# Modulation rows of PE copied by ACT and added in the column sums, loads in three parts, first column block formed by DVE and rounded from there

## What is computed

```python
c_act = jax.nn.silu(c)
mod = (c_act @ w_ada + b_ada)[:, None, :]
shift, scale, gate = jnp.split(mod, 3, axis=-1)
u = layer_norm(x) * (1 + scale) + shift
proj = u @ w_in + b_in
...
```

## Time and profile before

| what | us |
|---|---|
| median of 3 runs | 2171.29 |
| lowest and highest run | 2171.26, 2171.71 |
| the profiled execution | 2171.44 |
| its span, first to last instruction | 2169.3 |
| PE busy in the span | 2144.8 (99%) |
| PE weight loads busy | 1769.2 |
| DVE busy | 1270.0 |
| ACT busy | 784.7 |

### The profile page before, as it was taken

The page is one execution under the profiler, slowest core; times in us unless marked ns, Lnnn a source line. Parts: engine busy times, 40 slices in busy tenths (PEclk is TensorE's granted clock), DMA queues, the critical chain, the costliest instruction groups (busy, mean ns, idle before and its releaser), DMA issues.

```text
span 2169.3 us, 24997 instructions
## 1 busy us (share of the span) xinstructions
PE 2144.8 (99%) x10371; PEld 1769.2 (82%) x10371; DVE 1270.0 (59%) x1668; ACT 784.7 (36%) x1043; POOL 27.7 (1%) x41
## 2 busy tenths in 40 slices
PE   7999999999999999999999999999999999999998
PEld 4888888888888887888888888888788888888887
DVE  6899897944665848434665554234843466555423
ACT  3323232223343354344353333135534334333312
POOL 1000000000000100000000000000000000000000
PEclk9999999999999999999999999999999999999999
DMA  9432232232232222322223232222232222323322
GB/s 312 148 117 83 97 102 83 97 116 97 97 102 97 97 78 78 130 65 92 84 81 114 80 113 100 88 76 90 78 124 71 86 90 78 111 84 109 104 89 78
DMA packets 181364, 217.86 MB, mean 100 GB/s; under 512 B 3836, under 2 KB 152964, under 8 KB 180996
## 3 DMA queue, kind: packets, MB, share of 16 engines
q1 hardware_dynamic: 178000, 209.47, 29.2%
q10 hardware_dynamic: 2804, 4.65, 0.6%
q0 software_dynamic: 448, 2.15, 0.3%
HBM read 212.06 MB, written 4.19 MB: 100 GB/s over the span
## 4 chain that ended last, share of the span: by engine, by line
PE 96%; DVE 2%; DMA 1%; ACT 1%; issue 0%; POOL 0%; SPq 0%; POOLq 0%; ACTq 0%; DVEq 0%
PE psum L1790 30%; PE psum L1792 30%; PE psum L1791 30%; PE psum L2191 1%; DMA ada<-in_w_ada 1%; PE psum L2223 1%; PE psum L2203 1%; DVE whl L516 1%; PE psum L2157 1%; PE psum L2144 0%; PE psum L2176 0%; PE psum L1814 0%; POOL stat L677 0%; DVE hT L1474 0%; PE psum L2161 0%
## 5 line engine op out<-in xcount | busy, mean ns | idle before, releaser
L1790 PE MATMUL psum<-hT,whl 128*128 128x512 f32 (+1 forms) x2064 | 789.2, 382 | 3.3 <-DVE hT L1178 1.7
L1792 PE MATMUL psum<-hT,whl 128*128 128x512 f32 (+1 forms) x2064 | 783.2, 379 | 0.0
L1791 PE MATMUL psum<-hT,whl 128*128 128x512 f32 (+1 forms) x2064 | 783.0, 379 | 0.0
L516 DVE TENSOR_TENSOR whl<-raw,whl 128x1024 fp32r<-128x1024 f32 x361 | 438.2, 1216 | 430.8 <-ACT whl L509 430.6
L509 ACT ACTIVATE whl<-raw 128x1024 fp32r<-128x1024 f32 x362 | 377.7, 1047 | 425.1 <-PE psum L1792 385.6
L1790 PEld LDWEIGHTS psum<-hT,whl 128*128 128x128 f32 x2064 | 388.2, 188 | 84.6 <-issue 7.1
L1792 PEld LDWEIGHTS psum<-hT,whl 128*128 128x128 f32 x2064 | 388.3, 188 | 73.8
L1791 PEld LDWEIGHTS psum<-hT,whl 128*128 128x128 f32 x2064 | 388.4, 188 | 71.7 <-issue 0.2
L1790 PE MATMUL psum<-whl,ff 128*128 128x512 f32 x352 | 137.1, 389 | 0.0
L1792 PE MATMUL psum<-whl,ff 128*128 128x512 f32 x352 | 136.9, 389 | 0.0
L1791 PE MATMUL psum<-whl,ff 128*128 128x512 f32 x352 | 136.9, 389 | 0.0
(11 more groups left out here) (320 smaller groups left out, 2159.5 us busy)
## 6 DMA issues: line engine op xcount, KB each, us to landing
raw<-in_w_in SPq DMA_DIRECT2D x88, 1024.0 KB, 5.1
raw<-in_w_up SPq DMA_DIRECT2D x44, 1024.0 KB, 5.1
raw<-in_w_down SPq DMA_DIRECT2D x20, 1024.0 KB, 5.0
ada<-in_w_ada SPq DMA_DIRECT2D x12, 1024.0 KB, 10.9
raw<-in_w_branch SPq DMA_DIRECT2D x12, 1024.0 KB, 4.9
raw<-in_w_out SPq DMA_DIRECT2D x12, 1024.0 KB, 5.0
x<-in_x SPq DMA_DIRECT2D x4, 512.0 KB, 6.2
v_by_token<-vnat ACTq DMA_DIRECT2D x4, 512.0 KB, 3.0
```

The lines of the kernel that those rows point to most:

```text
L516: nc.vector.tensor_tensor(whl_view(w, 1), raw_view(w), whl_view(w, 0).bitcast(F), ALU.subtract).then_inc(w_lo, 1)
L1790: M(out_, stat_hi, mov_hi, start=start, stop=False, **kw)
L1791: M(out_, stat_hi, mov_lo, start=False, stop=False, **kw)
L1792: return M(out_, stat_lo, mov_hi, start=False, stop=stop, **kw)
```

## The change

Four things change together.

1. PE's row no longer goes into `adsum`. ACT copies it from PSUM into `table[0:1, i % 2, :]` (`row_copy`), and `ada_columns` adds it there: after each matmul of 128 rows a second one follows on the same PSUM column, whose weights are 128 columns of that single row and whose moving operand is one number. DVE's addition (L1153) goes. All four rows now use the same PSUM partition, so `ada_product(i)` waits until the row before has been copied.
2. PE's share of row groups by block goes from 3, 5, 3, 3 to 4, 4, 2, 3 in the order 0, 2, 1, 3.
3. Each block comes in three loads, `k` 0 to 3, 4 and 5, 6 and 7, each with its own semaphore, and DVE waits for them one by one.
4. For column block 0 DVE forms the full value first (`u_whole`, semaphore `first_u`), ACT rounds it from `utmp` to the high part, and DVE subtracts. ACT does its part of block 1 after that.

```diff
-    PE_ROWS = {0: 3, 2: 5, 1: 3, 3: 3}
+    PE_ROWS = {0: 4, 2: 4, 1: 2, 3: 3}
...
-                for q in (2 * b, 2 * b + 1):
-                    k0, n0 = q % 2 * 4, b * SEQ
-                    sp.dma_start(ada[:, q, :].rearrange("p (k n) -> p k n", k=4), wa[:, k0:k0 + 4, n0:n0 + SEQ]).then_inc(s_ada[q], 16)
+                both = ada[:, 2 * b:2 * b + 2, :].rearrange("p q (k n) -> p (q k) n", k=4)
+                for i, (k0, k1) in enumerate(((0, 4), (4, 6), (6, 8))):
+                    sp.dma_start(both[:, k0:k1, :], wa[:, k0:k1, b * SEQ:(b + 1) * SEQ]).then_inc(s_ada[b][i], 16)
...
+            def row_copy(i):
+
+                act.wait_ge(arow_ps, i + 1)
+                A(table[0:1, i % 2, :], bank(7)[0:1, :], ACT.Copy).then_inc(s_arow, 1)
...
+                if ct == 0:
+                    act.wait_ge(s_u0, 1)
+                    A(hT[:, 0, 0, :], utmp[:, 0, :], ACT.Copy).then_inc(h_hi, 1)
+                    return
...
-                weighted(part, lambda k: ada_rows(b, k), range(PE_ROWS[b], KT)).then_inc(s_part, 1)
-                dve.wait_ge(s_part, i + 1)
-                dve.wait_ge(arow_ps, i + 1)
-                own = part[32 * b:32 * b + 1, :]
-                V.tensor_tensor(own, own, bank(7)[32 * b:32 * b + 1, :], ALU.add).then_inc(s_adsum, 1)
+                for k in range(PE_ROWS[b], KT):
+                    if k == PE_ROWS[b] and k < 4:
+                        dve.wait_ge(s_ada[b][0], 16)
+                    if k in (4, 6):
+                        dve.wait_ge(s_ada[b][k // 2 - 1], 16)
...
+                ins.then_inc(s_adsum, 1)
...
+                if i:
+                    pe.wait_ge(s_arow, i)
...
                 pe.wait_ge(s_adsum, i + 1)
+                pe.wait_ge(s_arow, i + 1)
                 for m in range(4):
-                    ins = M(bank(6)[:, 4 * b + m:4 * b + m + 1], adsum[:, 2 * b + m // 2, m % 2 * P:(m % 2 + 1) * P], negones[:, 0:1],
-                            start=True, stop=True)
+                    o_ = bank(6)[:, 4 * b + m:4 * b + m + 1]
+                    M(o_, adsum[:, 2 * b + m // 2, m % 2 * P:(m % 2 + 1) * P], negones[:, 0:1], start=True, stop=False)
+                    ins = M(o_, table[0:1, i % 2, m * P:(m + 1) * P], negones[0:1, 0:1], start=False, stop=True)
```

More of the change, by code:

```diff
@@ L387, in build @@
         s_vec, s_vec2, s_cst, s_cst2, s_adag, s_bcast = (sem(n) for n in ("vec_in", "vec2_in", "cst_in", "cst2_in", "adag_in", "bcast_in"))
-        s_ada = [sem(f"ada_in{q}") for q in range(8)]
+        s_ada = [[sem(f"ada_in{b}_{i}") for i in range(3)] for b in range(TB)]
         s_c, s_cT, u_act = sem("c_in"), sem("c_transposed"), sem("u_by_act")
-        arow_ps, s_part, s_nmr, s_xc = sem("ada_row_psum"), sem("ada_part"), sem("neg_mean_rstd"), sem("x_columns")
+        arow_ps, s_arow, s_u0, s_nmr, s_xc = sem("ada_row_psum"), sem("ada_row_copied"), sem("first_u"), sem("neg_mean_rstd"), sem("x_columns")
         s_vT, s_vcol, s_mod, s_modc, s_gp, s_gate = (sem(n) for n in ("vecT", "vcol_ready", "mod_psum", "modc_ready", "gate_psum", "gate_ready"))
@@ L705, in _ @@
                 A(xn1[:, tb, :], x[:, tb, :], ACT.Identity, bias=nmr[:, tb:tb + 1], scale=rstd[:, tb:tb + 1]).then_inc(s_xn, 1)
+            def row_copy(i):
+                act.wait_ge(arow_ps, i + 1)
+                A(table[0:1, i % 2, :], bank(7)[0:1, :], ACT.Copy).then_inc(s_arow, 1)
+            row_copy(0)
             act.wait_ge(s_vT, 6)
@@ L711, in _ @@
             A(halfb[:, 96:128], vcol[:, VOFF["b_gate"]:VOFF["b_gate"] + 32], ACT.Copy, scale=0.5).then_inc(s_ini, 1)
+            row_copy(1)
             split_hi(0)
             def columns_hi(ct):
+                if ct == 0:
+                    act.wait_ge(s_u0, 1)
+                    A(hT[:, 0, 0, :], utmp[:, 0, :], ACT.Copy).then_inc(h_hi, 1)
+                    return
                 act.wait_ge(s_xc, ct + 1)
@@ L728, in _ @@
             columns_hi(3)
-            for w in range(2, 6):
-                split_hi(w)
+            split_hi(2)
+            split_hi(3)
+            row_copy(2)
+            split_hi(4)
+            split_hi(5)
+            row_copy(3)
             act.wait_ge(s_modc, 2)
@@ L1144, in ada_sum @@
                 b = MOD_ORDER[i]
-                if PE_ROWS[b] < 4:
-                    dve.wait_ge(s_ada[2 * b], 16)
-                dve.wait_ge(s_ada[2 * b + 1], 16)
                 part = adsum[:, 2 * b:2 * b + 2, :].rearrange("p a b -> p (a b)")
-                weighted(part, lambda k: ada_rows(b, k), range(PE_ROWS[b], KT)).then_inc(s_part, 1)
-                dve.wait_ge(s_part, i + 1)
-                dve.wait_ge(arow_ps, i + 1)
-                own = part[32 * b:32 * b + 1, :]
-                V.tensor_tensor(own, own, bank(7)[32 * b:32 * b + 1, :], ALU.add).then_inc(s_adsum, 1)
+                for k in range(PE_ROWS[b], KT):
[3 more added lines that the diff above has]
+                        dve.wait_ge(s_ada[b][k // 2 - 1], 16)
+                    if k == PE_ROWS[b]:
+                        ins = V.tensor_scalar(part, ada_rows(b, k), cact[:, k:k + 1], None, ALU.mult)
+                    else:
+                        ins = V.scalar_tensor_tensor(part, ada_rows(b, k), cact[:, k:k + 1], part, ALU.mult, ALU.add)
+                    if k < KT - 1:
+                        link(ins)
+                ins.then_inc(s_adsum, 1)
             def modulation(h):
@@ L1166, in u_whole @@
                 dve.wait_ge(s_xc, ct + 1)
-                if ct >= 2:
-                    dve.wait_ge(h_lo, ct - 1)
+                u = lambda: V.tensor_scalar(utmp[:, 0, :], bank(X_BANK[ct]), modc[:, 8 + ct:9 + ct], modc[:, ct:ct + 1], ALU.mult, ALU.add)
+                if ct == 0:
+                    u().then_inc(s_u0, 1)
+                    return
+                dve.wait_ge(h_lo, ct - 1)
                 dve.wait_ge(h_hi, ct + 1)
-                modulated[ct] = step(V.tensor_scalar(utmp[:, 0, :], bank(X_BANK[ct]), modc[:, 8 + ct:9 + ct], modc[:, ct:ct + 1], ALU.mult, ALU.add))
+                modulated[ct] = step(u())
             def u_lo(ct):
@@ L1174, in u_lo @@
                     dve.wait_ge(u_act, ct // 2 + 1)
-                else:
+                elif ct:
                     dve.wait_ge(dve_chain, modulated[ct])
@@ L1929, in ada_product @@
                 b = MOD_ORDER[i]
+                if i:
+                    pe.wait_ge(s_arow, i)
                 for k in range(PE_ROWS[b]):
-                    if k % 4 == 0:
-                        pe.wait_ge(s_ada[2 * b + k // 4], 16)
-                    ins = M(bank(7)[32 * b:32 * b + 1, :], cact[:, k:k + 1], ada_rows(b, k), start=k == 0, stop=k == PE_ROWS[b] - 1)
+                    if k == 0:
+                        pe.wait_ge(s_ada[b][0], 16)
+                    ins = M(bank(7)[0:1, :], cact[:, k:k + 1], ada_rows(b, k), start=k == 0, stop=k == PE_ROWS[b] - 1)
                 ins.then_inc(arow_ps, 1)
```

## The result

The changed kernel took 2180.52 us (median of 5 runs, 2178.88 to 2180.86) against 2171.71 for the kernel before in the same comparison: ratio 1.0038, 95% interval 1.0027 to 1.0049, 8.8 us slower. 2178.8 was forecast, within 2174.0 to 2182.0. The sum was close; two of its terms were not, in opposite directions, so that the closeness is partly luck. The trace shows which.

A forecast was written before the change was run, and what follows sets the result against it. PE was taken to bound the kernel, being 96% of its chain. Modulation +3.7, first block +0.5, product 2 -0.9 and columns 2 and 3 +4.2 gave +7.5 us on 2171.29, so 2178.8, range 2174.0 to 2182.0.

The forecast's parts named there:

- PE, not DVE, sets the modulation: Before the first tile: DVE's sum done at 23.8, columns 0 starting at 23.7, both `ada_columns` then shifting the modulation +3.7 us.
- The price of an `ada_columns`: Sixteen alternating records on PE: 1.82 us plus eight row changes at 0.15, so 3.0 us, between 2.5 and 3.3.
- s: Price of one change between 128-row and one-row weights in an `ada_columns`: between 0.09 and 0.19 us, taken as 0.15.
- the row at 19.05: Vector transposes before: going from 128-row to 32-row weights took 0.30 against 0.11, the 0.19 us upper bound per change.
- the lower bound of 0.09: Least price of one row change, from the second block: first matmul with 4-row weights 0.31 after the previous, against 0.23.
- The clock: Rival: single-column matmuls and short transposes before the first tile lower PE's clock; 2180.8 to 2182; 0.13, shared with dearer change.
- a dearer change: Rival: each row change in `ada_columns` waits for a whole record, 3.8 us per block, +10.7, 2182; 0.13 including clock.
- C: Time of one `ada_columns` on PE after the change: forecast 3.0 us, between 2.5 and 3.3.
- The first block: Column block 0: DVE forming first makes ACT's later steps late, so PE's tile 1 starts 0.5 us later.
- Product 2 and the later queue: PE from tile 1 on: product 2 loses one row group, -0.88 us; nothing new is late around block 3.
- No price for changing rows: Rival: row changes in `ada_columns` are free, 1.82 us per block, +2.8 us, 2174.1; chance 0.15, including prices under 0.05.
- PE follows DVE: Rival: one-row matmuls hidden behind the others, `ada_columns` stays 0.91 us, sum -0.9, 2170.4; chance 0.04.

The follow-up runs named there:

- e2: Changed kernel with each `ada_columns` reordered: four matmuls of 128 rows first, then the four of one row; 2176.39 us, ratio 1.0021 to the kernel before.
- e1: Changed kernel with the one-row matmuls taking 128 rows of `table`, 127 of them zero; 2174.73 us, ratio 1.0014 to the kernel before.
- e4: Kernel before with part 4 alone: DVE forms column block 0's full value first, ACT rounds from there; 2172.18 us, ratio 1.0001.
- e10: Kernel before with the four matmuls of the third and fourth `ada_columns` run three times over; 2178.54 us, ratio 1.0029.
- e6: Changed kernel with the four pairs of the third `ada_columns` placed between tile 4's row groups; 2179.03 us, ratio 1.0033 to the kernel before.
- e3: Changed kernel with part 1 undone: no ACT copies, DVE adds PE's row into `adsum` as before; 2171.26 us, ratio 0.9998 to the kernel before.
- e5: Changed kernel with part 4 undone: ACT rounds column block 0 from PSUM as before; 2180.14 us, ratio 1.0036 to the kernel before.

## Why the prediction was right, point by point

**PE, not DVE, sets the modulation.** Right. Columns 0 start at 24.01 (23.7 forecast, 23.90 before), DVE's sum is done at 24.0 (23.8 forecast), and DVE then waits 5.3 us. ACT's copies, at 19.71 and 24.11 in the profile after, hold nobody up.

**The price of an `ada_columns`.** The mechanism was right, its size too dear: 2.48 us and not 3.0. The step that failed is the choice of s. I took 0.15, nearer to the row at 19.05; it measured 0.084, a hair under the lower bound of 0.09 that came from the second block's 0.31 against 0.23. The account that I gave for the lower bound (where loads set the pace, an exposed load is in the pace already) gives this size. What made the row at 19.05 dearer no run shows; that the matmul before it moves 128 columns and not one may be the reason. In the sum: 4 x (3.0 - 2.48) = 2.1 us too much.

Of the two rules of the Trainium skill, the one in "TensorE: Matmul & The Clock Gate", section LDWEIGHTS, says that a load's time follows its columns and not its rows. The trace agrees: eight one-row records take 0.97 us and eight of 128 rows 0.99 (e2). The other, in "TensorEngine Tiling (Array Packing)" of the Trainium skill, section Key Properties, has a drain at a change of the tiling mode, without a price. That a change from 128 rows to one is such a change no run here shows; what the runs show is that each costs 0.08 us (e1, e2).

**The clock.** I gave its fall together with a dearer change 0.13, and in the profiled execution it fell three times. This is the term that was missing in the sum. The price can be read from like stretches: tile 4 took 4.32 us (52.73 to 57.05) where it took 2.86 (47.62 to 50.48), 1.46 more; eight transposes 1.62 and not 1.0, tile 5 3.62 and not 2.83, together 1.4; before the first tile some 0.7, of which 0.2 lie in the last pair of columns 1 (29.17 - 28.66 = 0.51 where a pair takes 0.31) and 0.5 in the first four transposes (DVE takes up the first block 1.23 after they begin, 0.75 in e4). About 3.6 us in all. With C = 2.48 my formula gives 4C - 4.5 = +5.4. Columns 0 began at 24.01 and not at 23.7, 0.3 more, and with the 3.6 that is +9.3; the profiled execution is 2180.68 - 2171.44 = +9.2, by the spans 9.6. So it was luck that the time came out near the forecast: one term was 2.1 too large, and another, which I held for unlikely, was 3.6 and stood at nothing in the sum. A forecast by the best numbers without the clock would have been 2176.7.

I had counted the stretch before the first tile alone as a danger; two of the three falls, 2.9 of the 3.6 us, came behind columns 2 and 3, between full tiles, which I had not counted. My sign for it, matmuls of the first tile 0.46 apart, was no good either: they start at 32.81, 33.11 and 33.35, since the clock fell in the transposes ahead of them and was back. e10 shows that a longer run of single-column matmuls is enough for a fall, e6 that with full ones between them it stayed away in tile 4; e3 shows a fall behind a wait of PE, without part 1.

**The first block.** Right in sign and place, 0.5 forecast, 0.64 measured alone (e4) and about 0.6 in the changed kernel (e5).

**Product 2 and the later queue.** Right: from 35.64 to 39.98 and on to tile 2 at 41.78, PE's lag sinks from 4.28 to 3.42, by 0.86, where 0.88 was forecast for one row group. No new wait appeared at block 3's loads.

**The rivals.** "No price for changing rows" is what e1 makes of the kernel: 2174.73, with one fall of the clock in its trace, where 2174.1 had been worked out without one. "PE follows DVE" had no cover, and none appeared.

## What to carry to other kernels

Before work is moved from an engine that waits to the one that it waits for, write down when each of them would be ready after the move: here DVE became 1 us earlier and PE 3 us later. A matmul that moved a single column cost its weight load here, 0.12 us a record, whatever its rows, and a change of the number of rows cost 0.08 again; the row was added more cheaply where it lay in a full-height tile (e1), or before the tile was summed (e3). Keep runs of such matmuls short or part them by full ones: they kept PE busy in the profile, and its clock fell behind them all the same.

## What the runs showed of the hardware

- A PE without a gap in its timeline can lose its clock. In e10 it stood at 1.00 through product 3, then came 2.7 us of single-column matmuls, and from the third pass to 53.3 those behind them ran 0.43 apart, with a granted clock of 0.59 in the stretch from 49.4 to 53.0, against 0.23 and 1.00 in the kernel before.
- The start of the clock shows in the times. The granted clock of product 0's stretch reads 1.00, but its first records are 0.85 apart, and how many of them are slow differs between executions: the eight records of product 0 took 5.81 us in the profile after, 5.32 in e1 and 6.45 in e6, and columns 0 began at 24.01, 23.57 and 24.64. In the profile before, product 1 waits 0.22 for its load after it, and only that much is hidden: in e10, which is the kernel before up to columns 2, product 0's six records took 5.28 and not 4.71, and columns 0 began at 24.38 and not at 23.90.
- The kernel before may lose its clock at times as well: of its 63 executions in the comparisons of the experiments, 16 have a span some 1.6 us longer than the others (2170.7 to 2171.2 against 2169.2 to 2169.8) and a mean granted clock of 0.998, not 0.999 or 1.0. No trace of one of these was kept, so what costs them the time stays open; the readings of before in this document come from an execution of 2169.3.
- A change between 128-row and one-row weights costs 0.08 us where weight loads set the pace and the matmuls move one column.
